# Three of the eight weight units of the first modulation as column products on TensorE, and another order of the first loads

## The reference

```python
mod = jax.nn.silu(c) @ w_ada + b_ada
shift, scale, gate = jnp.split(mod, 3, axis=-1)
h = _rmsnorm(x, norm_g) * (1.0 + scale[:, None, :]) + shift[:, None, :]
proj = h @ w_in
```

## Time and profile before

| what | value |
| --- | --- |
| runs | 3064.76, 3061.47, 3064.49 us |
| median | 3064.49 us |
| span of the profiled execution | 3060.0 us |
| TensorE busy in the span | 3000.5 us |
| VectorE (DVE) busy | 1887.5 us |
| ScalarE (ACT) busy | 1288.2 us |
| first product of the projections begins | 41.78 us after the span's start |

### The profile page before, as it was taken

One profiled execution on the slowest core, in us unless ns is written; L12 is line 12 of the kernel. 1 busy time (PEld: TensorE's weight loads), 2 busy tenths in 40 slices (PEclk: granted clock), 3 DMA queues, 4 the chain that ended last, 5 costly groups with the idle time before them and its releaser, 6 DMA issues. The chain is left out here.

```text
span 3060.0 us, 43842 instructions
## 1 busy us (share of the span) xinstructions
PE 3000.5 (98%) x17652; PEld 2538.7 (83%) x17652; DVE 1887.5 (62%) x2718; ACT 1288.2 (42%) x2007; POOL 1083.3 (35%) x798
## 2 busy tenths in 40 slices
PE   8999999999999999999999999999999999999998
PEld 6887878788777789988867899978999786789996
DVE  7476244837524277854475777757785437577775
ACT  4356442436553243423473534334343347443432
POOL 2443445525353422225341322252222544132222
PEclk8999999999999999999999999999999999999999
DMA  6223315313231232222210233223322221023321
GB/s 272 104 84 110 100 44 199 138 63 112 96 112 44 83 114 103 104 80 82 82 43 28 104 104 104 97 76 114 104 96 87 80 83 42 29 104 104 104 97 49
DMA packets 57442, 288.66 MB, mean 94 GB/s; under 512 B 6776, under 2 KB 7288, under 8 KB 30200
## 3 DMA queue, kind: packets, MB, share of 16 engines
q1 hardware_dynamic: 54000, 270.32, 25.1%
q10 hardware_dynamic: 3240, 15.53, 1.6%
HBM read 283.67 MB, written 2.16 MB: 93 GB/s over the span
## 5 line engine op out<-in xcount | busy, mean ns | idle before, releaser
L143 POOL TENSOR_TENSOR w_parts<-w_raw,w_parts 128x512 fp32r<-128x512 f32 x380 | 542.0, 1457 | 714.3 <-ACT w_parts L132 691.4
L395 PE MATMUL PS<-x_parts,w_parts 128*128 128x512 f32 x2784 | 688.3, 394 | 2.7 <-ACT m_all L1398 1.6
L395 PEld LDWEIGHTS PS<-x_parts,w_parts 128*128 128x128 f32 x2784 | 517.8, 188 | 117.6 <-issue 12.5
L2143 POOL TENSOR_TENSOR partial_parts<-ffn_buffers,partial_parts 128x512 fp32r<-128x512 f32 x128 | 186.2, 1456 | 727.6 <-ACT partial_parts L2338 727.6
L2184 PE MATMUL PS<-hidden_parts,partial_parts 128*128 128x512 f32 x1536 | 372.5, 392 | 0.0
L2184 PEld LDWEIGHTS PS<-hidden_parts,partial_parts 128*128 128x128 f32 x1536 | 280.6, 189 | 52.6
L2164 PE MATMUL PS<-x_parts,w_parts 128*128 128x512 f32 x1152 | 264.6, 391 | 1.0 <-POOL x_parts L847 1.0
L2164 PEld LDWEIGHTS PS<-x_parts,w_parts 128*128 128x128 f32 x1152 | 215.3, 188 | 50.2 <-POOL x_parts L847 1.8
L132 ACT CAST w_parts<-w_raw 128x2048 fp32r<-128x2048 f32 (+1 forms) x92 | 172.1, 1870 | 160.5 <-PE PS L395 73.2
L2202 PE MATMUL PS<-x_parts,w_parts 128*128 128x256 f32 x1536 | 205.2, 284 | 0.0
L2202 PE MATMUL PS<-x_combined_parts,w_parts 128*128 128x256 f32 x1536 | 204.9, 283 | 0.0
(11 more groups left out here) (440 smaller groups left out, 5010.5 us busy)
## 6 DMA issues: line engine op xcount, KB each, us to landing
w_raw<-in_w_gu SPq DMA_DIRECT2D x88, 1024.0 KB, 4.8
w_raw<-in_w_in SPq DMA_DIRECT2D x70, 1024.0 KB, 4.8
ffn_buffers<-in_w_part SPq DMA_DIRECT2D x128, 256.0 KB, 2.7
w_raw<-in_w_out SPq DMA_DIRECT2D x24, 1024.0 KB, 4.8
m_all<-in_w_next SPq DMA_DIRECT2D x14, 1024.0 KB, 8.3
w_raw<-in_w_last SPq DMA_DIRECT2D x12, 768.0 KB, 4.2
m_all<-in_w_gate SPq DMA_DIRECT2D x8, 1024.0 KB, 4.8
ssd_buffers<-decay_rows ACTq DMA_DIRECT2D x16, 512.0 KB, 3.8
```

Of the source, the lines that this page charges most:

```text
L143: pool.tensor_tensor(parts[:, self.slot(u), 1, at:to], raw[:, self.slot(u), at:to], parts[:, self.slot(u), 0, at:to].bitcast(F32), ALU.sub ...
L395: return pe.matmul(PS[0:m, self.bank(j), :], w[w_][:, k, c:c + m], part(x_, k), start=start, stop=stop)
L2143: pool.tensor_tensor(small_parts[:, d % 2, 1, :], small_raw[:, d % 2, :], small_parts[:, d % 2, 0, :].bitcast(F32), ALU.subtract).then_inc ...
```

## The change

Units 2, 4 and 6 of the modulation no longer go to DVE. They hold the same 768 outputs in another layout (`w_mod`: 128 input features by 256 outputs for each of eight feature tiles). TensorE multiplies each 128 by 128 piece, as the stationary operand, with one column of `c_columns`, a small array of 128 by 8 that is loaded and put through silu on its own. That is 16 products a unit, accumulated over eight tiles into two columns of PSUM bank 1; DVE copies the six columns out at the end. The five row units stay on DVE.

TensorE's order becomes: four fillers, column unit 2, the sums of squares, column unit 4, the spread of the inverse root with its two fillers, column unit 6, three fillers.

The loads are reordered. SP: `c_row`, units 0, 2, 3, then (after unit 0 was used) unit 4 and the first projection unit, units 5, 6, 7 as slots come free, `par` after unit 5, then `c1` and the second projection unit as before. ACT: `c_columns`, positions, constants, unit 1, `x`. At its end SP waits for the three column units too, and the start of the angle chain, of the fillers and of the silu of the columns now waits for all three loads counted in `s_in`.

```diff
             def sums(self, pe, sq):
-                keep_busy(pe, 2, 6)
                 for k in range(KD):
...
                 last.then_inc(self.spread, 1)
+
+            def spread_out(self, pe):
                 pe.wait_ge(self.moved, 1)
                 self.spread_inverse(pe, 2)
-                keep_busy(pe, 2, 4)
...
+            UNITS = ("row", "row", "column", "row", "column", "row", "column", "row")
+            product = PS[:, 1, 0:2 * n_columns]
...
                 sp.dma_start(B.c_row, dr["c_row"]).then_inc(s_c, 16)
-                sp.dma_start(cst[:, :], dr["c0"]).then_inc(s_in, 16)
-                for u in (0, 2):
-                    sp.dma_start(ring[:, u, :], ada_rows(0, u)).then_inc(s_nl[u], 16)
+                for u in (0, 2, 3):
+                    sp.dma_start(ring[:, u, :], unit_rows(u)).then_inc(s_nl[u], 16)
+                sp.wait_ge(*used(0))
+                sp.dma_start(ring[:, 0, :], unit_rows(4)).then_inc(s_nl[0], 16)
                 stream.send(sp, RAW, 1)
-                for u in range(4, NEARLY):
-                    sp.wait_ge(s_nu, 2 * (u - 3))
...
+                for u in range(5, NEARLY):
+                    sp.wait_ge(*used(u - 4))
...
                 sp.wait_ge(s_c1, 16)
+                sp.wait_ge(s_np, n_columns)
...
-                pe.wait_ge(s_in, 32)
+                def columns(u):
+                    pe.wait_ge(s_nl[u % 4], 16 * (u // 4 + 1))
+                    w = split3(ring[:, u % 4, :], KD)
+                    for n in range(2):
+                        at = 2 * nth[u] + n
+                        for k in range(KD):
+                            last = pe.matmul(product[:, at:at + 1], w[:, k, n * P:(n + 1) * P], c_columns[:, k:k + 1],
+                                             start=(k == 0), stop=(k == KD - 1))
+                    last.then_inc(s_np, 1)
+
+                pe.wait_ge(s_in, 48)
+                keep_busy(pe, 2, 4)
+                pe.wait_ge(s_cc, 1)
+                columns(2)
                 norm.sums(pe, B.squares)
+                columns(4)
+                norm.spread_out(pe)
+                columns(6)
+                keep_busy(pe, 2, 3)
...
+                act.dma_start(c_columns, dr["c_columns"]).then_inc(s_in, 16)
                 act.dma_start(posi, dr["pos"]).then_inc(s_in, 16)
-                act.dma_start(ring[:, 1, :], ada_rows(0, 1)).then_inc(s_nl[1], 16)
+                act.dma_start(cst[:, :], dr["c0"]).then_inc(s_in, 16)
+                act.dma_start(ring[:, 1, :], unit_rows(1)).then_inc(s_nl[1], 16)
                 act.dma_start(x_all[:, :], dr["x"]).then_inc(s_x, 16)
-                act.dma_start(ring[:, 3, :], ada_rows(0, 3)).then_inc(s_nl[3], 16)
                 act.wait_ge(s_c, 16)
                 act.activation(B.c_row, B.c_row, ACT.Silu).then_inc(s_cr, 1)
+                act.wait_ge(s_in, 48)
+                act.activation(c_columns, c_columns, ACT.Silu).then_inc(s_cc, 1)
...
+                rows(0)
+                rows(1)
+                dve.wait_ge(s_sin, 2)
+                link(dve.tensor_scalar(SIN, SIN, const("sign"), None, ALU.mult))
+                rows(3)
+                stream.lower(dve, RAW, WP, 1)
+                rows(5)
+                norm.invert(dve)
+                rows(7)
+                dve.wait_ge(s_np, n_columns)
+                link(dve.tensor_copy(raw_mod[:, 2 * n_rows:16], product))
```

More of the change, by code:

```diff
@@ L3257, in setup @@
             s_cr, s_nu, s_mod = sem("c_row_activated"), sem("ada_used"), sem("modulation_ready")
+            s_cc, s_np = sem("c_columns_activated"), sem("column_units_done")
             posi = B.early[:, 0:T].bitcast(I32)
@@ L3260, in setup, with unit_rows, used @@
             ring = split3(m_all[:, :], 4)
+            c_columns = mod[:, 32:40]
+            UNITS = ("row", "row", "column", "row", "column", "row", "column", "row")
+            nth = [UNITS[:u].count(UNITS[u]) for u in range(NEARLY)]
+            n_rows, n_columns = UNITS.count("row"), UNITS.count("column")
+            product = PS[:, 1, 0:2 * n_columns]
+            def unit_rows(u):
+                return ada_rows(0, nth[u]) if UNITS[u] == "row" else dr["w_mod"][nth[u]]
+            def used(u):
+                return (s_nu, 2 * (nth[u] + 1)) if UNITS[u] == "row" else (s_np, nth[u] + 1)
             @block.sync
@@ L3302, in _ @@
                 link = chain(dve, s_vc)
-                dve.wait_ge(s_in, 32)
+                dve.wait_ge(s_in, 48)
                 link(dve.tensor_copy(ang, posi))
@@ L3323, in rows @@
                 def rows(u):
+                    n = nth[u]
                     dve.wait_ge(s_nl[u % 4], 16 * (u // 4 + 1))
[L3325 to L3336, removed]
+                    dot_rows(dve, ring[:, u % 4, :], B.scratch, B.c_row, raw_mod[:, 2 * n:2 * n + 2], s_nu, 2 * n)
+                rows(0)
[9 more added lines that the diff above has]
+                link(dve.tensor_copy(raw_mod[:, 2 * n_rows:16], product))
+                dve.wait_ge(s_nu, 2 * n_rows)
                 dve.wait_ge(s_par, 16)
@@ L3340, in _ @@
                 dve.wait_ge(s_c1, 16)
-            return s_nu
+            return s_nu, 2 * n_rows
         def clear_at_once():
@@ L3360, in build @@
             used = under(own[0], setup, block, streams, norm, B)
-            under(own[0], retention, block, 0, streams, Modulated(norm, 2), B, (used, 2 * NEARLY))
+            under(own[0], retention, block, 0, streams, Modulated(norm, 2), B, used)
         own += [Scope() for _ in range(4)]
@@ L3545, in layout @@
     d = dict(w_next=as_rows(a["w_ada"][:, :, 0:2 * D]), w_gate=as_rows(a["w_ada"][:, :, 2 * D:]),
+             w_mod=units(a["w_ada"][0:1], r(1280, 768), UC)[0], c_columns=column(a["c"])[0],
              c_row=np.broadcast_to(a["c"], (P, D)), w_in=halves(units(a["w_in"], cols, UC), (14, 16, 22, 24)),
```

4 lines of the change are left out of this document (2 added, 2 removed).

## The result

| kernel | median of its runs | runs |
| --- | --- | --- |
| before, same chip | 3064.62 us | 3061.47 to 3065.68 (4) |
| changed | 3077.52 us | 3076.93 to 3084.85 (4) |

The ratio is 1.0048 [1.0036, 1.0061]: the change costs 12.9 us. 3075.8 was predicted, with 3067 to 3081 as the range.

What follows compares the result with a forecast made beforehand. TensorE was busy 3000.5 of 3060.0 us, with DVE setting the first projection's start. First product +13.0, less 1.7 back in `begin`, is 11.3; 3060.0 + 11.3 = 3071.3, with the median 4.5 above: 3075.8, range 3067 to 3081.

Steps and rivals of the forecast that it cites:

- `begin`: First projection stage, first product to third job: 12.6 us before, predicted 10.9, giving 1.7 back.
- fillers of step 1: Four fillers opening TensorE's order: eight records, four slow at 0.86 us and the others 0.43, 5.2 us.
- fillers of step 5: Two fillers behind the spread on TensorE: 2.7 us, between all-fast and all-slow records.
- the predicted gap before the sums: TensorE's wait for the squares of `x` behind column unit 2, about 1 us, from 20.6 to 21.6.
- Packets in turn, not bytes: How the DMA queues share: by packet, constants land at 11.0; by bytes, 6.4, the lower end.
- The 4.5 us from the span to the median: Added to the predicted profiled execution, 3071.3, because the median stood that far above the span: 3075.8.
- Two side sums: Load landings from bytes moved: unit 7 at 32.7 after 12.3 MB, first projection unit near 27 after 9.7 MB.
- Its saving: DVE's relief from three units: done by 38, it then waits 12 us for TensorE, so worth nothing.
- SP's held-back loads: Gate units and third projection unit, held until 50.5 by SP's last wait, land about 60, still ahead of use.
- The clock stays up: Rival, not slower: column products and sums all at the upper clock level, -0.2 us, 3064.3; chance 0.12.
- TensorE is never late: Rival, faster: DVE sets the start at about 36.3 us, 2.9 sooner with `begin` 4.6, 3059.9; chance 0.03.
- Everything late: Rival, slower still: constants later, column units and fillers wholly at the lower clock, 3081.8; chance 0.06.

Runs made afterwards that it cites:

- e3: The changed kernel with two products in each column unit instead of 16; 3067.02 us, ratio 1.001 to the kernel before.
- e4: The changed kernel without the three fillers behind column unit 6; 3074.45 us, ratio 1.0037 to the kernel before.
- e5: The changed kernel with column products turned round, repeated column of `c` stationary and weights streaming; 3080.23 us, ratio 1.0019 to the kernel before.
- e6: The changed kernel with column products and sums of squares both turned into wide products, without spread and later fillers; 3078.69 us, ratio 1.001 to before.
- e9: The changed kernel run and profiled again, unaltered, on another chip; 3075.53 us, ratio 1.0039 to the kernel before.
- e1: The kernel before with only the new order of loads, all eight units on DVE; 3072.73 us, ratio 1.0033 to the kernel before.
- e11: The changed kernel with a wait that keeps POOL from starting its twelve products beside the long DVE instruction; 3076.35 us, ratio 1.0043 to before.
- e8: The kernel before with only the first-loaded unit as one-column products, old load order, one ACT rounding moved; 3076.15 us, ratio 1.0008 to before.

## Why the prediction was right

The mechanism was the predicted one in the predicted order: TensorE becomes the bound of the setup stage, through one-column products at the lower clock. The steps, as the prediction numbered them:

| step | predicted | changed kernel |
| --- | --- | --- |
| constants | 11.0 | 11.8 |
| 1 fillers | 5.2 | 6.4 |
| 2 column unit 2 | 4.4, to 20.6 | 4.1, to 22.3 |
| 3 `x`; sums | 20.8; 21.6 to 34.9 | 21.3; 22.3 to 35.9 |
| 4 column unit 4 | 6.6 | 6.8 |
| 5 spread; fillers | 1.9; 2.7 | 1.8; 3.4 |
| 6 column unit 6 | 4.4, to 50.5 | 3.6, to 51.6 |
| 7 first product | 54.8 (+13.0) | 55.6 (+13.8) |
| `begin` | 10.9 | 11.3 |
| third job | 65.7 (+11.3) | 66.9 (+12.5) |

Shown by the experiments: the products' own work is 9.8 us of it (`e3`), the end fillers are neutral because the first records run at the lower level otherwise (`e4`), and the same arithmetic in a form that holds the clock about halves the loss (`e5`, `e6`). The terms off by the most are the fillers of step 1 (1.2 short: six records ran at the slow pace where four were counted), the fillers of step 5 (0.7 short) and the constants (0.8), against unit 6 (0.8 too much). That the total is off by only 1.2 us is in part luck: the predicted gap before the sums took up 1 us of the delay of the first steps, and unit 6 offsets the fillers of step 5. One execution of the same kernel differs from another by as much: in the second profile (`e9`) the gap was there and the third job began at 65.58, against the 65.7 predicted. Packets in turn, not bytes, was the right reading for the constants: sharing by bytes would have given 6.4.

The 4.5 us from the span to the median are no fixed offset of the profiler: in the runs with both numbers the time lies 1.7 to 1.9 above the span (3084.85 over 3083.1), and the rest was the profiled execution of before being one of its fastest. The sum is not touched by this, since it comes to the median of before plus 11.3, and with the measured third job 3064.6 + 12.5 = 3077.1 against 3077.5.

Two side sums of the prediction don't come out at its own 424 GB/s: 12.3 MB before unit 7's landing give 32.0 us and not 32.7, and 9.7 MB put the first projection unit at 25.8 and not near 27 (ACT began to round it at 27.7). Neither enters the forecast.

DVE and SP went as predicted. The last row unit ended at 39.1 (37.9 predicted) and DVE waited 12.67 us (12). Its saving was worth nothing: its later start and its own waits had used it up before the wait for TensorE began, and that wait would have swallowed it anyway. SP's held-back loads cost nothing either: the gate units were issued at 52.0, TensorE's third job had no wait, and the lag did not grow for the next 800 us. The prediction had both waits of DVE, for the first projection unit and for the root, in its sum, but gave the new order no price of its own. With all eight units on DVE it costs 8.8 us (`e1`); in the change that is hidden because TensorE is later still.

The rivals. "The clock stays up" failed in its main condition, that the level holds through the sums. The gap that was held against it does not decide this: in the first profile there was none and the clock fell within column unit 2, and in the second the level outlived the gap of 1.06 us and fell 0.65 us into the sums (window from 21.95 to 22.60 at 1.00, from 22.60 to 34.95 at 0.50). The Trainium skill ("TensorE: Matmul & The Clock Gate", Part 1) says that sustained matmul activity releases the throttle; taken to include one-column products, that does not agree with 0.50 through 13.7 us of them without a pause, while wide products (`e6`) held 1.00 over much the same stretch (22 to 36 us). "TensorE is never late" failed by 12.67 us. "Everything late" came true in its small parts (constants, fillers) and not in the large ones (units 2 and 6).

## What to carry to other kernels

An engine that is idle is not free: before moving work to it, price the new form by a row of that form in that state. Here the row was a run of one-column products at half clock, and it priced a unit at 6.6 us (6.8 came) against 2.5 on DVE. In this kernel a vector times a matrix was better with the vector as the repeated stationary operand and the matrix streaming: at the upper level both forms took 3.6 us a unit, but only the streaming one brought the clock back and held it. But count what the next engine pays to use a result that stands on all partitions. And when a slot of a ring is given back by another engine than before, look at which loads queue behind that one on the issuer.

## What was not expected of the hardware

- One DVE product of 128 by 512, beside POOL's row of twelve products without a pause, took 12.84 us in some executions and 1.66 in others of the same code (0.69 when POOL stood still). It ended at 980.82, just behind the last of POOL's twelve (980.27). TensorE waited 9.0 us behind it and its clock fell (0.51 from 976.6 to 980.0), and on one chip runs moved in steps of about 11 us. That the kernel before had it as well is inferred from its groups of runs, since its profile has none; what starts it is open.
- Small DVE instructions stretch beside POOL: the 128 by 16 sum took 0.17 us alone, 1.11 in `e1` and 1.26 in `e6`, both while POOL lowered weights.
- Whether a clock level of 1.00 that fillers had raised survives 32 one-column records is not fixed by their place in the code. Column unit 2 of the change, directly behind four fillers, kept it in `e9` and `e11` (3.63 us in both) and lost it in its midst in the first profile and in `e4` (4.28 and 4.54). In `e8`, behind six fillers, it kept it (3.63). What decides it was not tested.
